# Retention projections in halves, spread over the MLA steps of a two-layer attention block, with the loads around them moved

## The reference

```python
for layer in range(DEPTH):
    h = _rms_norm(x, attn_norm[layer])
    (d_q, d_k, d_v, m_cq, m_ckv, m_krope,
     r_q, r_k, r_v, r_g) = _split_cols(h @ w_in[layer])
    ...
    o_diff = _diff_attention(d_q, d_k, d_v, ...)
    o_mla = _mla(m_cq, m_ckv, m_krope, ...)
    o_ret = _retention(r_q, r_k, r_v, r_g, ...)
    mixed = jnp.concatenate([o_diff, o_mla, o_ret], axis=-1)
    x = x + mixed @ w_out[layer]
    h = _rms_norm(x, ffn_norm[layer])
    x = x + (jax.nn.silu(h @ w_gate[layer]) * (h @ w_up[layer])) @ w_down[layer]
return _rms_norm(x, final_norm)
```

## Time and profile before

| | |
|---|---|
| median of 3 runs | 2634.92 us (2629.35 to 2635.21) |
| the profiled execution | 2631.62 us |
| its span on the core | 2629.7 us |
| TensorE busy | 2537.3 us, 96% |
| VectorE, ScalarE, GpSimd busy | 58%, 42%, 38% |
| mean load of the 16 DMA engines | 92 GB/s |

### The profile page before, as it was taken

The page is one execution under the profiler, slowest core; times in us unless marked ns, Lnnn a source line. Parts: engine busy times, 40 slices in busy tenths (PEclk is TensorE's granted clock), DMA queues, the critical chain, the costliest instruction groups (busy, mean ns, idle before and its releaser), DMA issues. The chain is left out here.

```text
span 2629.7 us, 43301 instructions
## 1 busy us (share of the span) xinstructions
PE 2537.3 (96%) x13164; PEld 2176.6 (83%) x13164; DVE 1538.0 (58%) x3049; ACT 1094.5 (42%) x2510; POOL 1009.1 (38%) x1150
## 2 busy tenths in 40 slices
PE   6999999999999999999999999999999999999997
PEld 6999977778788888888889998777887888888886
DVE  4666655472655445577757765555637445445786
ACT  5444544362522232344445455444534332223444
POOL 3455522183244544201034554223823544451012
PEclk9999999999999999999999999999999999999999
DMA  5111011123233233573431101012222233327533
GB/s 183 30 35 46 11 36 39 43 72 136 63 116 108 80 115 108 191 257 97 120 97 32 35 20 41 6 39 91 97 80 89 80 115 108 112 83 273 184 99 120
DMA packets 238699, 242.68 MB, mean 92 GB/s; under 512 B 27953, under 2 KB 171057, under 8 KB 238513
## 3 DMA queue, kind: packets, MB, share of 16 engines
q1 hardware_dynamic: 237984, 238.34, 28.4%
q10 hardware_dynamic: 528, 2.10, 0.2%
HBM read 172.75 MB, written 67.63 MB: 91 GB/s over the span
## 5 line engine op out<-in xcount | busy, mean ns | idle before, releaser
L2559 POOL TENSOR_TENSOR fw_a_lo<-fw_a_raw,fw_a_hi 128x512 fp32r<-128x512 f32 x132 | 178.8, 1355 | 456.0 <-DVE fw_s_raw L2133 456.0
L2559 POOL TENSOR_TENSOR fw_s_lo<-fw_s_raw,fw_s_hi 128x512 fp32r<-128x512 f32 x176 | 231.4, 1327 | 54.5 <-ACT fw_s_hi L1607 54.5
L753 PE MATMUL banks<-ht_hi,da_hi 128*128 128x512 f32 x496 | 193.1, 389 | 0.0
L753 PE MATMUL banks<-ht_hi,da_lo 128*128 128x512 f32 x496 | 193.0, 389 | 0.0
L753 PE MATMUL banks<-ht_lo,da_hi 128*128 128x512 f32 x496 | 193.0, 389 | 0.0
L753 PE MATMUL banks<-w_diff_hi,ht_hi 128*128 128x384 f32 x512 | 179.6, 351 | 2.3 <-DVE dv L1844 2.0
L753 PE MATMUL banks<-w_diff_hi,ht_lo 128*128 128x384 f32 x512 | 171.9, 336 | 0.0
L753 PE MATMUL banks<-w_diff_lo,ht_hi 128*128 128x384 f32 x512 | 171.6, 335 | 0.0
L2387 POOL TENSOR_TENSOR qk_rot<-rope_a,rope_b 128x512 f32<-128x512 f32 x64 | 82.5, 1292 | 194.7 <-DVE rope_b L1830 175.7
L1865 DVE TENSOR_REDUCE stats<-banks 128x1 f32<-128x1024 f32 (+3 forms) x192 | 138.4, 748 | 28.3 <-PE banks L988 22.4
L1681 ACT ACTIVATE u_two<-u_two 128x512 f32<-128x512 f32 x42 | 26.6, 632 | 280.8 <-DVE u_two L2244 280.8
(11 more groups left out here) (368 smaller groups left out, 7475.6 us busy)
## 6 DMA issues: line engine op xcount, KB each, us to landing
da_raw<-act_scratch SPq DMA_DIRECT2D x154, 256.0 KB, 2.7
fw_a_raw<-in_w_gate_dram SPq DMA_DIRECT2D x88, 256.0 KB, 3.1
act_scratch<-act_s SPq DMA_DIRECT2D x66, 256.0 KB, 3.0
w_diff_raw<-in_w_in_dram SPq DMA_DIRECT2D x24, 512.0 KB, 6.1
fw_a<-in_w_up_dram SPq DMA_DIRECT2D x44, 256.0 KB, 3.2
fw_a_raw<-in_w_up_dram SPq DMA_DIRECT2D x44, 256.0 KB, 2.9
act_scratch<-act_zero SPq DMA_DIRECT2D x44, 256.0 KB, 2.4
act_scratch<-act_one SPq DMA_DIRECT2D x44, 256.0 KB, 2.8
```

What stands on the lines that cost most here:

```text
L753: mm = pe.matmul(bank, lhsT, rhs, start=first and i == 0, stop=last and i == len(pairs) - 1, skip_group_check=resumes)
L2559: pool.tensor_tensor(w[1][:], w[2][:], w[0][:].bitcast(F32), ALU.subtract).then_inc(S["f_lo"], 1)
```

## The change

1. `ret_part_at` replaces the map of units by a map of halves. Pair 0: one half in each of steps 4 to 9, two in each of steps 10 to 14. Pair 1: one half in each of steps 19 to 22, two in each of steps 23 to 28. A lone half stands at the first place of its step. `ROUND_RET` stays.
2. The waits for weights are split by half for the retention chunks: first half for parts 0 and 1 of the rounding, second half for all four. Only the first unit of a pair waits for them.
3. Pair 1's weights are loaded by contraction halves (8 transfers of half the size), the second half after unit 10's store.
4. The first output columns are issued by ScalarE after it has taken the last projected unit (`load_first_output_columns`). `causal`, `gn_w` and `gn_b` stay on SP, after unit 28's store instead of unit 25's.
5. `mixed_rows` is loaded in three pieces: columns 0 to 511 of tokens 0 to 511 after unit 29's store and the last scores, of tokens 512 to 1023 after unit 30's store and the last output product, columns 512 to 767 after all stores.

```diff
-        ret_unit_at = {(7 if n < T else 13) + n: n for n in range(RET_UNITS)}
+        ret_part_at = {}
+        for first, steps in ((0, [*range(4, 10), *(a for a in range(10, 15) for _ in range(2))]),
+                             (T, [*range(19, 23), *(a for a in range(23, 29) for _ in range(2))])):
+            for i, a in enumerate(steps):
+                ret_part_at.setdefault(a, []).append((first + i // 2, i % 2))
+        ret_unit_at = {a: n for a, parts in ret_part_at.items() for n, part in parts if part == 1}
...
+        def lo_count(chunk, half=1):
+            return chunk + 1 + (0 if chunk < CH_RET else chunk - CH_RET + half if chunk < CH_OUT else RET_PAIRS)
...
+                def load_second_ret(half):
+                    k = slice(half * KD // 2, (half + 1) * KD // 2)
+                    src = w_in[L].rearrange("(k p) n -> p k n", p=P)
+                    for i in range(4):
+                        start = COL_RET + i * RET_W + P
+                        arrives(w_ret[2][:, k, i * P:(i + 1) * P], src[:, k, start:start + P], f"w_in{1 - half}")
...
+                def load_diff_rows(half):
+                    for i in range(2):
+                        sp.wait_ge(S[f"mix_out{i}"], L * PER[f"mix_out{i}"] + 16 * DIFF_HEADS * T // 2)
+                    tiles = slice(4 * half, 4 * half + 4)
+                    arrives(mixed_rows[:, tiles, 0:MIX_MLA], mixed_dram.rearrange("(t p) d -> p t d", p=P)[:, tiles, 0:MIX_MLA], f"mix_in{half}")
...
                             sp.wait_ge(S["z_done"], L * PER["z_done"] + Z_RET + T)
-                            load_ret(1)
-                        if h * T + T - 1 - t == 25:
+                            load_second_ret(0)
+                        if h * T + T - 1 - t == 10:
+                            load_second_ret(1)
+                        if h * T + T - 1 - t == 29:
+                            sp.wait_ge(S["s_done"], L * PER["s_done"] + PER["s_done"])
+                            load_diff_rows(0)
+                        if h * T + T - 1 - t == 30:
+                            sp.wait_ge(S["pv_done"], L * PER["pv_done"] + PER["pv_done"])
+                            load_diff_rows(1)
+                        if h * T + T - 1 - t == 28:
                             sp.wait_ge(S["z_done"], L * PER["z_done"] + Z_UNITS)
-                            load_out(0)
                             arrives(causal[:], causal_dram, "ret_in")
...
-                arrives(mixed_rows[:, :, 0:MIX_RET], mixed_dram.rearrange("(t p) d -> p t d", p=P)[:, :, 0:MIX_RET], "mix_in")
+                arrives(mixed_rows[:, :, MIX_MLA:MIX_RET], mixed_dram.rearrange("(t p) d -> p t d", p=P)[:, :, MIX_MLA:MIX_RET], "mix_in2")
...
                     for part in parts:
+                        if chunk >= CH_RET and t == 0:
+                            pe.wait_ge(S["w_hi"], L * PER["w_hi"] + PARTS * chunk + PARTS // 2 * (part + 1))
+                            pe.wait_ge(S["w_lo"], L * PER["w_lo"] + lo_count(chunk, part))
...
-                def ret_project(a, part):
-
-                    if a in ret_unit_at:
-                        n = ret_unit_at[a]
+                def ret_project(a, place):
+
+                    for n, part in ret_part_at.get(a, [])[place:place + 1]:
                         project(Z_RET + n, n % T, CH_RET + n // T, w_ret, 4 * P, (part,))
...
                         act.activation(r_z[n][:], banks[:, Z_BANK, :], ACT.Copy).then_inc(S["z_free"], 1)
+                        if n == RET_UNITS - 1:
+                            load_first_output_columns()
+
+                def load_first_output_columns():
+                    act.dma_start(w_o[0][2][:], w_out[L].rearrange("(k p) n -> p k n", p=P)[:, :, 0:512]).then_inc(S["w_in0"], 16)
```

More of the change, by code:

```diff
@@ L126 @@
 PER = dict(
-    params_in=16 * 8, ret_in=16 * 3, x_saved0=16, x_saved1=16, x_back0=16, x_back1=16, mix_in=16,
-    w_in0=16 * (3 + 3 + 1 + 4 + 4 + 1), w_in1=16 * (3 + 3 + 4 + 1), w_gain=1, w_hi=PARTS * CHUNKS, w_lo=CHUNKS,
+    params_in=16 * 8, ret_in=16 * 3, x_saved0=16, x_saved1=16, x_back0=16, x_back1=16, mix_in0=16, mix_in1=16, mix_in2=16,
+    w_in0=16 * (3 + 3 + 1 + 4 + 4 + 1), w_in1=16 * (3 + 3 + 4 + 4 + 1), w_gain=1, w_hi=PARTS * CHUNKS, w_lo=CHUNKS + RET_PAIRS,
     lam=5, n_sq=2 * T, n_ms=5, n_rstd=5, n_xn=2 * T, tr_done=RING, tr_hi=RING - NORM2_RINGS - MLA_HEADS * T, tr_free=RING - 1,
@@ L482, in hybrid_block_kernel @@
         RET_UNITS = RET_PAIRS * T
-        ret_unit_at = {(7 if n < T else 13) + n: n for n in range(RET_UNITS)}
+        ret_part_at = {}
[4 more added lines that the diff above has]
+        ret_unit_at = {a: n for a, parts in ret_part_at.items() for n, part in parts if part == 1}
+        assert sorted(ret_unit_at.values()) == list(range(RET_UNITS))
         ROUND_RET = (0, 16)
@@ L547, in load_diff, with load_ret @@
                     load_columns(h, w_diff[h % 2][2], [c + h * P for c in (COL_DQ, COL_DK, COL_DV)], P)
-                def load_ret(p):
-                    load_columns(CH_RET + p, w_ret[2], [COL_RET + i * RET_W + p * P for i in range(4)], P)
-                def load_out(c):
-                    arrives(w_o[c][2][:], w_out[L].rearrange("(k p) n -> p k n", p=P)[:, :, c * 512:(c + 1) * 512],
-                            f"w_in{c}")
+                def load_ret():
+                    load_columns(CH_RET, w_ret[2], [COL_RET + i * RET_W for i in range(4)], P)
+                def load_second_ret(half):
[4 more added lines that the diff above has]
+                        arrives(w_ret[2][:, k, i * P:(i + 1) * P], src[:, k, start:start + P], f"w_in{1 - half}")
                 def save_rows(half):
@@ L607, in _ @@
                 sp.wait_ge(S["z_done"], L * PER["z_done"] + Z_MLA + T)
-                load_ret(0)
+                load_ret()
                 for h in range(MLA_HEADS):
@@ L799, in project @@
                     if 0 in parts:
-                        pe.wait_ge(S["w_hi"], L * PER["w_hi"] + PARTS * (chunk + 1))
-                        pe.wait_ge(S["w_lo"], L * PER["w_lo"] + chunk + 1)
+                        if chunk < CH_RET:
+                            pe.wait_ge(S["w_hi"], L * PER["w_hi"] + PARTS * (chunk + 1))
+                            pe.wait_ge(S["w_lo"], L * PER["w_lo"] + lo_count(chunk))
                         if u > T:
@@ L1080, in mixed_block @@
                 def mixed_block(half, k):
-                    pe.wait_ge(S["mix_in"], L * PER["mix_in"] + 16)
+                    arrived = f"mix_in{half}" if k < MIX_MLA // P else "mix_in2"
+                    pe.wait_ge(S[arrived], L * PER[arrived] + 16)
                     if mixed_ring[0] > freed[0]:
@@ L1099, in first_product @@
                             pe.wait_ge(S["w_hi"], L * PER["w_hi"] + PARTS * (CH_OUT + 1))
-                            pe.wait_ge(S["w_lo"], L * PER["w_lo"] + CH_OUT + 1)
+                            pe.wait_ge(S["w_lo"], L * PER["w_lo"] + lo_count(CH_OUT))
                         if i == 0 and mixed_ready[k] > freed[0]:
@@ L1197, in last_blocks @@
                     pe.wait_ge(S["r_mx"], L * PER["r_mx"] + T // 2 + 2 * half + 2)
-                    transpose_rows(mixed_rows[:, 4 * half:4 * half + 4, :], "mix_in", 16, range(KD - 2, KD), n_banks=2)
+                    transpose_rows(mixed_rows[:, 4 * half:4 * half + 4, :], "mix_in2", 16, range(KD - 2, KD), n_banks=2)
                     return ring[0]
@@ L1212, in _ @@
                             pe.wait_ge(S["w_hi"], L * PER["w_hi"] + PARTS * (CH_OUT + 2))
-                            pe.wait_ge(S["w_lo"], L * PER["w_lo"] + CH_OUT + 2)
+                            pe.wait_ge(S["w_lo"], L * PER["w_lo"] + lo_count(CH_OUT + 1))
                         pe.wait_ge(S["out_add"], L * PER["out_add"] + q - 3)
@@ L1325, in round_weights @@
                 def round_weights(chunk, n_in, parts, whole=PARTS):
-                    act.wait_ge(S[f"w_in{slot(chunk)}"], L * PER[f"w_in{slot(chunk)}"] + n_in)
+                    if chunk != CH_RET + 1:
+                        act.wait_ge(S[f"w_in{slot(chunk)}"], L * PER[f"w_in{slot(chunk)}"] + n_in)
                     for hi, raw in parts:
@@ L1353, in weights @@
                         w, n = w_ret, (11, 15)[chunk % 2]
+                        if chunk == CH_RET + 1 and 0 in parts:
+                            act.wait_ge(S["w_in1"], L * PER["w_in1"] + 16 * 14)
+                        if chunk == CH_RET + 1 and PARTS // 2 in parts:
+                            act.wait_ge(S["w_in0"], L * PER["w_in0"] + 16 * n)
                     else:
-                        w, n = w_o[chunk % 2], (16, 11)[chunk % 2]
+                        w, n = w_o[chunk % 2], (16, 15)[chunk % 2]
                     step = KD // PARTS
@@ L2376, in weights @@
                         st = pool.tensor_tensor(w[1][:, k, :], w[2][:, k, :], w[0][:, k, :].bitcast(F32), ALU.subtract)
-                        if i == PARTS - 1:
```

(1 more changed line is left out.)

2 lines of the change are left out of this document (1 added, 1 removed).

## The result

The changed kernel takes 2647.44 us at the median (2646.90 to 2647.89), the kernel before on the same chip 2633.65: a ratio of 1.0051, 95% interval 1.0039 to 1.0063. It is slower, by half a percent, and the interval leaves out 1. The prediction of 2624.3 us, with its range of 2616 to 2633, did not hold; a time more than 8 us above the kernel before had been given a chance of 0.05, all of it from rival D, which is not what happened. The profiled execution has a span of 2645.7 us, 16.0 more than before; its last matmul starts at 2630.89 instead of 2614.89.

The account below looks back on a forecast made before the run. TensorE, busy 96% of the span, was taken as the bound, so only its idle time could be won: 2 x (-3.35) + 2 x 1.14 - 6.2 = -10.6 us, giving a median of 2624.3 us, range 2616 to 2633.

Parts of the forecast that it names:

- rival D: Slower: unit 29's store, behind the small tables on SP's queue, lands late and holds GpSimd; 2636.5 us, chance 0.08.
- Is one half (2.8 us) enough cover?: Steps 7 to 9, left one half each: holes average 1.1 us, well under a half, so no new wait.
- rival E: Cover too short: holes return in steps 7 to 9 and the first pair gains nothing; 2631 us, chance 0.1.
- the 5.18 us: Steps 4 to 6 without halves, taken from steps 12 to 14: 5.18 of their 8.53 us, leaving a 3.35 us hole.
- -2.21: Steps 19 to 22: gain per layer from filled holes and an earlier first product, if rounding comes as early as now.
- +1.14: Second pair, net per layer: -2.00 and -0.21 us gained, +3.35 us new wait for weights in step 20.
- the signs of being wrong: Listed: no idle in step 20, long m_mx wait for a store, holes in steps 7 to 9, clock drop elsewhere.
- Rival C: No wait in step 20, ScalarE's rounding coming before its transposes' turn; 2617.6 us, chance 0.1.
- The end of the stage: Output columns off SP's queue bring the retention's first transpose 3.4 and 2.4 us earlier; 6.2 us over both layers.
- stores with nothing ahead on their own queue take some 1.5 us: End of the stage: units 26 and 27's stores need not wait out the 2 MB; 1.5 us is the median store.
- Rival B: Shared engines: stores crawl beside another queue's 2 MB, only the projections' -4.4 us is left; 2630.5 us, chance 0.25.
- TensorE did not stand for them: Mixed rows: TensorE did not wait for the late 3 MB, so loading them in three pieces is worth zero.

Follow-up runs that it names:

- the loads alone: Changed kernel with both pairs' halves back in steps 7 to 14 and 21 to 28, two a step, all changed loads kept: 2628.82 us, 0.9984.
- The order: Units as before, all changed loads, but the 2 MB of output columns back on SP's queue behind unit 25's store: 2631.06 us, 0.9986.
- the queue alone: Kernel before with only the first output columns issued by ScalarE behind the last retention unit: 2629.28 us, 0.9976.
- the early rounding: Changed kernel with the second pair's weights rounded in steps 16 (two parts), 17 and 18 instead of 16 to 19: 2639.21 us, 1.0021.
- the rows in one: Kernel with lone halves behind the transposes and rounding in steps 15 to 18, its mixed_rows joined to one 3 MB transfer behind all stores: 2650.81 us, 1.0079.
- the kernel with halves behind and one rounding a step: Changed kernel with lone halves behind the transposes of probabilities and the second pair's weights rounded one part a step in steps 15 to 18: 2624.23 us, 0.9955.

## Why the prediction was wrong

**The first pair: wrong, and the step that failed is "Is one half (2.8 us) enough cover?"** It weighed the length of a hole (1.1 us) against the length of the half, and did not ask on which side of the transposes the half stands. What sets the length of such a step is the chain transposes, ScalarE, VectorE, transposes of queries: 2.10 us in step 5 before, 2.09 after. Work is covered by it only if it stands between the transposes and the matmul that waits for the chain. The change puts a lone half ahead of the transposes, where it adds its whole length less the wait for `m_out`. Forecast -3.35 us a layer, measured +2.2. Even the right place gives -1.4, for in step 9 the half that would cover the exponential is then missing: rival E, at a smaller price (1.8 us of its 3.35). Steps 12 to 14, from which the 5.18 us were drawn, have a half in both places, and so could not show which of the two does the covering.

**The second pair: the wait was right, the rest of the sum was mis-sized.** Forecast: a wait of 3.35 us in step 20; measured 3.4. Forecast for the holes: -2.21; measured with that placement +1.7, for the same reason as above, and -2.06 with the lone halves behind the transposes, once the weights are early. And "+1.14" left out what the wait sets off: the clock at 1.2 GHz, 2.4 us in layer 0 and 1.5 in layer 1. I had priced a fall of the clock at the end of the stage, where the trace showed one, and not at the place where I put a new and longer wait; a drop of the clock elsewhere stands only among the signs of being wrong. Together +7.4 and +6.6 instead of +1.14. Rival C, no wait, fell.

**The split load: right.** It costs nothing; marks 19 to 21 of the kernel with the loads alone are those of before.

**The end of the stage: right in the amount, in part by luck in the way.** -3.3 and -2.4 us against -3.4 and -2.4; the last transpose stands straight behind the seven fillers, and the granted clock stays at 1.00. The step that did not hold is that stores with nothing ahead on their own queue take some 1.5 us. In the changed kernel the stores of units 25 and 26 took 6.3 and 5.8 us beside the 2 MB, and only unit 27's, issued after they had landed, took 2.2. Rival B had this right, that stores crawl beside another queue's 2 MB, and was wrong that nothing is then gained: the 2 MB leave 1.9 us earlier, a term that neither it nor the prediction has. Rival D fell, for `gn_b` lands in 3.1 us; unit 29's store does stand behind the tables, and GpSimd waits 2.76 us for it (2.87 in layer 1), but behind the retention's first transpose; from there to layer 1's first mark the changed kernel takes only 0.45 us more (1647.05 - 532.71 against 1640.27 - 526.38). The order adds a share of its own: 1.8 and 0.6 us alone, and 0.6 and 0.5 on top of the queue.

**The mixed rows in three pieces: zero against the kernel before, but not worth nothing.** "TensorE did not stand for them" was true with 1.8 us to spare in layer 0, where they left at 528.18, landed near 539.8 and were wanted at 541.59, and with next to nothing in layer 1, where they landed at 1839.48 and were wanted at 1839.52. In the kernel with the queue alone they land at 538.3 and are wanted at 538.83. With the halves moved as well the 3 MB are late, and the pieces are worth 8.25 + 7.3 = 15.6 us between the two traces and 26.6 between the medians.

**Steps 1 to 3 of layer 1: not in the sum.** +2.6 us from a fall of the clock in a hole that the kernel before has as well. The fillers in it take it away. Why it comes stays open: of the traces without fillers in step 1, those of the changed kernel, the early rounding, the loads alone, the queue alone and the rows in one have it, the others do not. Nor is it shown that this hangs on the kernel. There is one trace of each, and the executions of the kernel before differ among themselves, with mean granted clocks of 0.993 to 0.998.

Between the profiled executions the error is 16.0 + 10.6 = 26.6 us (23.1 between the predicted and the measured median): 11.1 from the first pair, 11.8 from the second, 2.6 from steps 1 to 3, and about 1 from the rest. That the kernel with halves behind and one rounding a step took 2624.23 us, the predicted number, does not bear out its sum: there the first pair brings less than forecast and the second more. That the two cancel is chance.

## What to carry to other kernels

Filler work is free only between the instruction that starts a chain of dependent work and the one that waits for its end: before moving it, write down for each hole what opens it and what closes it, and look whether the steps taken as a model have filler on one side or on both. The wait that a profile names is the one that ended last; a chain just behind it can set the length once the first is gone. A new wait on TensorE is priced with the clock behind it, and where a wait can't be avoided, fillers ahead of it are worth their place. When an early stage is made shorter, look at every load with little to spare behind it; here a transfer had 1.8 us in one layer and 0.04 in the other. When a large transfer changes its queue, look first at when it now leaves, and read the small ones beside it from issue to landing: the wait for one of them alone misleads, as 2.57 instead of 6.34 us did here.

## What the runs showed of the hardware

A stand of TensorE of 1.4 us, among small matmuls and a few fillers, was followed by 17.1 us at 1.2 GHz; one of 3.1 us between dense matmuls by 6.8 us (3.4 in layer 1). The cost of a short wait thus lay mostly behind it: 1.4 us of waiting stood for 8.25 us of length. With 15 fillers in the place of the 3.1 us the clock did not fall. A short wait did not always have such an end: one of 1.26 us at 432.57, with one part of the rounding a step, was followed by full clock.

A store of 32 KB took 1.5 us from issue to landing with nothing large beside it. Issued some 4 us behind a transfer of 2 MB it took 5.2 to 5.4 us on the same queue and 5.4 to 5.8 us on another engine's, with the same small transfers around it. The 2 MB themselves took 7.7 to 9.6 us from ScalarE's queue and 9.0 to 9.4 from SP's.
